# Encoder trunk with seven-product matmuls: a second buffer for a weight sum, three reordered steps, one low part moved from POOL to VectorE

## The reference

```python
h = _rmsnorm(x, g_ffn[l])
z = _dwconv_centred(h @ w_up[l], conv_w[l], conv_b[l])
z_gate, z_val = jnp.split(z, [D_FF], axis=-1)
x = x + (jax.nn.silu(z_gate) * z_val) @ w_down[l]
```

## Time and profile before

| what | before |
|---|---|
| median of 3 runs | 1118.75 us |
| the profiled execution's own time | 1118.39 us |
| its span | 1116.6 us |
| TensorE busy | 1081.9 us (97%) |
| VectorE busy | 640.1 us (57%) |
| ACT busy | 556.4 us (50%) |
| POOL busy | 623.5 us (56%) |
| DMA, mean over the span | 120 GB/s |

### The profile page before, as it was taken

One profiled execution on the slowest core, in us unless ns is written; L12 is line 12 of the kernel. 1 busy time (PEld: TensorE's weight loads), 2 busy tenths in 40 slices (PEclk: granted clock), 3 DMA queues, 4 the chain that ended last, 5 costly groups with the idle time before them and its releaser, 6 DMA issues.

```text
span 1116.6 us, 18354 instructions
## 1 busy us (share of the span) xinstructions
PE 1081.9 (97%) x6492; PEld 952.3 (85%) x6492; DVE 640.1 (57%) x938; ACT 556.4 (50%) x772; POOL 623.5 (56%) x298
## 2 busy tenths in 40 slices
PE   9999999999998999999999999999998989998997
PEld 7788888887988989998878888888888988898987
DVE  5726755675476723766636377467636665146564
ACT  7835444544465524665557344354434654255651
POOL 5343244355888668875524323344459775687840
PEclk9999999999999999999999999999999999999999
DMA  8222223233856356652623222223357642765312
GB/s 305 86 93 79 74 76 106 84 95 116 221 138 156 107 156 156 157 137 76 180 77 95 77 77 62 90 79 109 96 167 172 154 129 77 206 171 150 95 57 76
DMA packets 40549, 134.35 MB, mean 120 GB/s; under 512 B 4752, under 2 KB 7568, under 8 KB 40464
## 3 DMA queue, kind: packets, MB, share of 16 engines
q1 hardware_dynamic: 32848, 107.03, 29.6%
q0 software_dynamic: 6912, 25.17, 12.6%
q10 hardware_dynamic: 704, 1.07, 0.3%
HBM read 122.76 MB, written 2.10 MB: 112 GB/s over the span
## 4 chain that ended last, share of the span: by engine, by line
PE 60%; DVE 12%; DMA 8%; POOL 8%; issue 5%; ACT 4%; DVEq 1%; ACTq 0%; SPq 0%; POOLq 0%
PE acc L1479 12%; PE acc L1480 11%; PE acc L1481 11%; POOL w_lo L454 6%; PE acc L1793 4%; PE acc L1796 4%; PE acc L1795 4%; DMA w_raw<-mixer_sb 4%; DVE arena L1281 3%; PE acc L1605 3%; PE acc L1607 3%; PE acc L1606 3%; DMA mixer_sb<-mixer_sb 2%; DVE mixer_sb L1307 2%; DMA w_raw<-slabs 2%
## 5 line engine op out<-in xcount | busy, mean ns | idle before, releaser
L464 POOL TENSOR_TENSOR w_lo<-w_raw,w_hi 128x1024 fp32r<-128x1024 f32 x108 | 261.3, 2425 | 334.9 <-ACT w_hi L521 329.0
L454 POOL TENSOR_TENSOR w_lo<-w_raw,w_hi 128x1024 fp32r<-128x1024 f32 x72 | 182.3, 2572 | 73.2 <-ACT w_hi L804 60.7
L1479 PE MATMUL acc<-feat_hi,w_hi 128*128 128x512 f32 (+1 forms) x496 | 190.1, 383 | 1.5 <-DVE x L1223 1.5
L1480 PE MATMUL acc<-feat_lo,w_hi 128*128 128x512 f32 (+1 forms) x496 | 189.6, 382 | 0.0
L1481 PE MATMUL acc<-feat_hi,w_lo 128*128 128x512 f32 (+1 forms) x496 | 189.6, 382 | 0.0
L521 ACT ACTIVATE w_hi<-w_raw 128x1024 fp32r<-128x1024 f32 x102 | 107.8, 1063 | 139.8 <-PE acc L1481 103.4
L1793 PE MATMUL acc<-xg_hi,w_hi 128*128 128x256 f32 x512 | 145.9, 285 | 4.5 <-DVE sides L1329 4.5
L1795 PE MATMUL acc<-xg_lo,w_hi 128*128 128x256 f32 x512 | 145.7, 285 | 0.0
L1796 PE MATMUL acc<-xg_hi,w_lo 128*128 128x256 f32 x512 | 145.5, 284 | 0.0
L1479 PE MATMUL acc<-xg_hi,w_hi 128*128 128x512 f32 x352 | 139.6, 397 | 0.0
L1480 PE MATMUL acc<-xg_lo,w_hi 128*128 128x512 f32 x352 | 137.1, 389 | 0.0
(11 more groups left out here) (177 smaller groups left out, 2171.4 us busy)
## 6 DMA issues: line engine op xcount, KB each, us to landing
w_raw<-slabs SPq DMA_DIRECT2D x166, 512.0 KB, 3.5
w_raw<-slabs POOLq DMA_DIRECT2D x16, 512.0 KB, 5.8
arena<-slabs SPq DMA_DIRECT2D x16, 512.0 KB, 5.0
arena<-slabs POOLq DMA_DIRECT2D x16, 512.0 KB, 6.4
mixer_sb<-slabs SPq DMA_DIRECT2D x8, 512.0 KB, 5.5
w_raw<-mixer_sb POOLq DMA_DIRECT2D x8, 512.0 KB, 6.4
mixer_sb<-mixer_sb POOLq DMA_DIRECT2D x8, 512.0 KB, 5.6
outT<-arena SPq DMA_DIRECT2D x7, 256.0 KB, 2.2
```

The source lines that it names most:

```text
L454: pool.tensor_tensor(w_lo[:, w], source, w_hi[:, w].bitcast(F32), ALU.subtract).then_inc(lo_done, 1)
L464: pool.tensor_tensor(w_lo[:, w], w_raw[:, w], w_hi[:, w].bitcast(F32), ALU.subtract).then_inc(lo_done, 1)
L1479: pe.matmul(out, wh, ah, start=first, stop=False)
L1480: pe.matmul(out, wh, al, start=False, stop=False)
```

## The change

```diff
@@ sb
+        second_s2 = sb("second_s2", [P, SLAB])
-        s2_raw = mixer_sb[:, SLAB:2 * SLAB]
+        s2_raw = [mixer_sb[:, SLAB:2 * SLAB], second_s2[:, :]]
@@ POOL: add_s4, low_quad
-                pool.dma_start(raw2[s % 2], s2_raw, accum_op=ALU.add).then_inc(s4_added[s % 2], 16)
+                pool.dma_start(raw2[s % 2], s2_raw[s % 2], accum_op=ALU.add).then_inc(s4_added[s % 2], 16)
                 low(n + S1_, raw1[s % 2])
+                if s < KP - 1:
+                    add_s1(L, p, s + 1)
                 low(n + A11_, raw0[s % 2])
                 add_s3(L, p, s)
-                if s < KP - 1:
-                    add_s1(L, p, s + 1)
                 low(n + A12_, raw2[s % 2])
                 add_s4(L, p, s)
-                low(n + S2_, s2_raw)
-                low(n + A22_, raw(3))
+                low(n + S2_, s2_raw[s % 2])
+                low_done(n + A22_)
                 low(n + S3_, raw0[s % 2])
@@ ACT: quad_step
                     high_s3(p, s)
                     if s:
                         silu(p, s - 1, 1)
-                        feat_high(p, s - 1, 0)
                     high_s4(p, s)
                     if s:
-                        feat_high(p, s - 1, 1)
+                        feat_high(p, s - 1, 0)
                         act.wait_ge(c12_added, quad_at(p, s))
                     copy(p, s, S2_, 1, u2_copy)
                     if s < KP - 1:
                         high_s1(p, s + 1)
+                    else:
+                        high_down(p, 0)
+                    if s:
+                        feat_high(p, s - 1, 1)
+                    if s < KP - 1:
                         high_a11(p, s + 1)
                     else:
-                        high_down(p, 0)
                         high_down(p, 1)
                     copy(p, s, S3_, 1, u3_copy)
@@ VectorE: add_s2, low_a22, convolve, quad_step
-                    if p or s:
-                        before = p * KP + s - 1
+                    if p * KP + s > 1:
+                        before = p * KP + s - 2
                         dve.wait_ge(s4_added[before % 2], 16 * (L * (QUADS // 2)) + 16 * (before // 2 + 1))
-                    dve.tensor_tensor(s2_raw, raw1[s % 2], raw0[s % 2], ALU.add).then_inc(s2_done, 1)
+                    dve.tensor_tensor(s2_raw[s % 2], raw1[s % 2], raw0[s % 2], ALU.add).then_inc(s2_done, 1)
+
+                def low_a22(p, s):
+
+                    unit = first_unit(p, s) + A22_
+                    w = slice((unit % RING) * SLAB, (unit % RING + 1) * SLAB)
+                    dve.wait_ge(hi_done, L * NU + (unit + 1))
+                    dve.wait_ge(lo_done, L * NU + (unit + RING))
+                    dve.tensor_tensor(w_lo[:, w], raw(3), w_hi[:, w].bitcast(F32), ALU.subtract).then_inc(lo_done, 1)
@@ convolve
                     taps(p, s, 0)
+                    if s < KP - 1:
+                        low_a22(p, s + 1)
                     scale(p, s, 3)
@@ quad_step
                     else:
+                        low_a22(p, 0)
                         add_s2(p, 1)
```

More of the change, by code:

```diff
@@ L823, in high_s2 @@
                     act.wait_ge(s2_done, L * QUADS + (p * KP + s + 1))
-                    high(first_unit(p, s) + S2_, s2_raw)
+                    high(first_unit(p, s) + S2_, s2_raw[s % 2])
                 def high_a22(p, s):
```

## The result

| | before | changed |
|---|---|---|
| median | 1119.81 us (4 runs) | 1102.84 us (4 runs, 1101.76 to 1105.94) |
| the profiled execution, its span | 1118.39, 1116.6 us | 1102.49, 1100.7 us |
| TensorE, VectorE, ACT, POOL busy | 1081.9, 640.1, 556.4, 623.5 us | 1074.2, 634.0, 558.2, 586.5 us |
| the four parts together | 360.8 us | 344.5 us |

The ratio is 0.9846, 95% interval 0.9811 to 0.9881: **faster by 17 us**, 1.5%, where 3.8 us were forecast.

The account below looks back on a forecast made before the run. TensorE's waits in the four up-projection parts (360.77 us, 38.2 lost) bound it; a new 22.6 us circle would leave 356.95, so 1118.39 - 3.8 + 0.36 = 1115.0 us, range 1107 to 1128.

Parts of the forecast that it names:

- the waits at S3: TensorE's waits of 2.69 us at a quad's sixth product, behind u2_copy on ACT; claimed to go.
- a circle: Low S2 on POOL, low_a22, scaling, centring, p1_copy, S3, back to low S2: 22.6 us a quad against TensorE's 20.16.
- the walk: Times of each step counted from the end of POOL's low S2 to the next quad's low S2, 22.6 us.
- Then A11, A12 and S2, each behind one DMA issue: 3.61 each: Last steps of POOL's round, from 11.8 us after low S2 to 22.6, in every quad.
- Is the clock lowered after 2.45?: TensorE's clock after a 2.45 us wait at S2: a drop counted, costing 1.58 us, 0.45 coming back into the round.
- 0.6 late already: Third up-projection part: S2 of its first quad was claimed 0.6 us late, at 844.7.
- The round, 22.6: Time from one quad's S2 to the next's: at least 22.6 us, 23.05 after a clock drop.
- The handover: From POOL's end of low S2 to VectorE's low_a22: 0.15 us taken, between 0.08 and 0.32.
- The signs named in advance: S2 waits by L865, rounds of 22.6, VectorE idle before low_a22, add_s2 under 1.5, POOL some 38 less, last part 87 us.
- the waits simply go: First rival: with a round under 20.16 us TensorE would run through, 1080.5 us; chance 0.08.
- The second and third: Rivals: POOL's subtractions lock out add_s2, for the run (1147 us, chance 0.07) or one instruction (1128, chance 0.05).
- The rule weighed in the sum: POOL and VectorE share an SBUF read port, so moving A22's low part might not help; port use 18.0 to 16.8 us.

Follow-up runs that it names:

- old_s1_place: The changed kernel with the DMA add of S1 back at its old place, right behind add_s3: 1102.73 us, ratio 0.9866 to the kernel before.
- copy_before_centring: The changed kernel with p1_copy and S3's high part put ahead of the third centring on ACT: 1080.51 us, ratio 0.9665 to the kernel before.
- only_buffer: The kernel before with the second S2 buffer alone: 1108.88 us, ratio 0.9912.
- only_act_order: The kernel before with ACT's new order alone (u2_copy ahead of the second feature's high part): 1096.89 us, ratio 0.9824.
- a22_on_pool: The changed kernel with the low part of A22 back on POOL: 1095.75 us, ratio 0.9807 to the kernel before.
- best_a22_on_pool: The changed kernel with p1_copy and S3's high part ahead of the third centring, and A22's low part back on POOL: 1110.45 us.
- issue_in_last: The changed kernel with one more 64 KB DMA issued by POOL in each part's last quad: 1104.07 us, ratio 0.9875 to the kernel before.
- old_act_order: The changed kernel with ACT's old order, both high parts of the features ahead of u2_copy: 1109.85 us, ratio 0.9927 to the kernel before.

## Why the prediction was wrong

Its mechanism held: the waits at S3 went, a circle took their place at S2, every link in the order given, and cutting one link (two variants) made it vanish. So did the direction. The sum was 356.95 us for the parts and 344.5 was measured, 12.4 less, beyond the bounds given. So the steps that failed are terms of the walk and of the clock, not its path. Four were off, sized here by comparing the forecast starts of S2, from each part's start, with the measured ones:

1. **"Then A11, A12 and S2, each behind one DMA issue: 3.61 each", used for the last quad too: 4.5 us.** No S1 follows a part's last quad; the line `if s < KP - 1` stands in the diff. Nor does an `add_s2` meet S3 there. The last rounds took 21.3 to 21.6 us instead of 22.6: 1.3 in parts 2 and 4, 1.0 in parts 1 and 3. One walk was made for a quad "that has one before it" and used three times.
2. **"Is the clock lowered after 2.45? ... so I count 1.58": 3.9 us.** It fell after the waits of 2.45 and 2.43 us at S2 of the second quad in parts 1 and 3, which the walk had as 2.8 and, by its own starts (868.7 where TensorE would have been there at 864.98), as 3.7. It did not after those of 2.18 and 2.16 in parts 2 and 4, nor after the last ones of parts 1 and 3, 1.4 us, which the walk's long last round had made 2.45. That is two drops at a part's end (3.0) and twice 0.45 in a round. Interpolating between two rows was the error, more than its result (see the last section).
3. **Part 3 "0.6 late already": 1.9 us.** The part's first DMA for S1 landed 5.7 us after its issue, not 7.3 as before, and the part began like part 1. S1's new place isn't the reason, since old_s1_place shows the same. What sped the transfer up stays open.
4. **The round, 22.6 for 22.4, and the first S2 that waits in parts 1, 2 and 4, forecast 0.3 to 0.4 too late: 2.1 us together.** The handover took 0.03 us where 0.15 was taken, below the lower bound of 0.08: bounds from other pairs of engines weren't bounds for this one. S1's issue doesn't wait for POOL's own subtraction, so it adds 0.9 and not 1.2 (458.47 to 459.07 above has no 0.30 before it; the L478 has). Against these, `add_s2` put low S3 back by 0.24 and not 0.06.

The signs named in advance came out so: rounds of 22.4 and 21.3 us instead of 22.6; twelve waits at S2 released by L865; idle time before L1319 (1.82 us above; 26.4 behind POOL in 14 waits); no `add_s2` over 1.5 us; POOL less busy by 37.0 us, forecast 38. The last part took 85.07 us, not 87, which points at terms 1 and 2.

Of the rivals, the first ("the waits simply go") gave 1080.5 and needed a circle under 20.16 us. It has 1080.51 in copy_before_centring; the prediction saw the link that stood in the way but had no reason to weigh it as removable. The second and third, the lock-out of `add_s2`, did not happen in the changed kernel, because VectorE had only the taps in front, as argued. They happened in only_buffer, only_act_order, a22_on_pool and best_a22_on_pool, up to 12.7 us. On the third, the Trainium skill, SBUF — State Buffer, SBUF: two separate sides, has the one that started first hold the shared ports for one whole instruction: 3.35 us in only_act_order fit it, the 8.23 above do not.

The rule weighed in the sum, the Trainium skill's Perfetto Trace Analysis, Optimizing Scalar/DVE Operations (work moved between these two engines might bring nothing), doesn't settle it here: the same move costs 7 us in one order of ACT and brings 30 in the other. By these runs it depends on whether the piece falls into a pause of POOL and on what is queued behind it.

## What to carry to other kernels

When a piece of work moves to another engine behind a wait, follow what is queued behind it on that engine around until it comes back to whoever ends the wait; if the way round is longer than the period, cut it at the cheapest link, here by putting one copy and one high part ahead of a centring. Walk the first and the last turn of a loop by themselves, since guards such as `if s < KP - 1` take work out of them. And try each piece of a change alone and left out: here three pieces alone gave some 10, 6 and 20 us by their ratios, together 17, and with the circle cut 38.

## What the runs showed of the hardware

**VectorE can be kept out for a whole run of POOL's subtractions, and not only for one.** Over all fourteen traces 55 `add_s2` took more than 1.6 us. The 31 of up to 3.46 us met one subtraction. The 24 from 4.9 to 12.7 us met two to five, and every one of those began 0.2 to 0.37 us before the last had ended, as the rows at 317.40, 319.76 and 322.14 do. Two make 4.9 to 5.5 us, three 6.2 to 8.0, four 8.2 to 10.0, five 12.7. All 24 stood in a run without a pause behind a DMA issue of POOL. Most of the 31 were let in where POOL's next subtraction still had to wait, or where a DMA issue came next. But eight were not: there the next subtraction was free to go, and the sum got in ahead of it all the same. The rows of only_act_order above are one of them: ACT's high part, for which POOL's subtraction at 448.49 had to wait, was done at 447.52.

```profile
446.47 1.05 ACT L804 ACTIVATE w_hi<-mixer_sb 128x1024 fp32r<-128x1024 f32 x1
```

In those eight the run had begun, 0.04 to 1.1 us before the sum, with a subtraction that POOL itself had waited for. So a pause lets VectorE in, but a missing pause doesn't always keep it out; whether it is the DMA issue at the head of the run that does, no experiment here has tried.

**The length of a wait doesn't by itself decide whether TensorE's clock falls.** Two waits of issue_in_last, at S2 of the third quad in parts 2 and 4, and the 24 matmuls behind each; then two of old_act_order, in part 4 (columns of the stretches as above):

```profile
474.29 0.39 PE L1812 MATMUL acc<-t_hi,w_hi 128*128 128x256 f32 x1 [1.99 <-ACT arena L869]
1015.70 0.39 PE L1812 MATMUL acc<-t_hi,w_hi 128*128 128x256 f32 x1 [2.00 <-ACT arena L869]
...
474.29:478.75 4.46, 4.46 (x24) 4.46 (x25) 4.19 (x6) 2.84 (x4) 3.43 (x2) 0.62 0.30 111
1015.70:1018.67 2.97, 2.97 (x24) 2.97 (x25) 2.83 (x4) 2.85 (x4) 1.93 (x1) 1.00 0.44 163
```

```profile
1019.06 0.39 PE L1805 MATMUL acc<-t_hi,w_hi 128*128 128x256 f32 x1 [2.71 <-ACT arena L865]
1041.47 0.39 PE L1805 MATMUL acc<-t_hi,w_hi 128*128 128x256 f32 x1 [1.86 <-ACT arena L865]
...
1019.06:1022.03 2.97, 2.97 (x25) 2.97 (x26) 2.83 (x4) 2.55 (x4) 1.94 (x1) 1.00 0.34 134
1041.47:1045.93 4.46, 4.46 (x24) 4.46 (x25) 3.53 (x6) 3.44 (x5) 3.42 (x2) 0.62 0.14 53
```

Equal waits went both ways: a mean granted clock of 0.62 over the product after 1.99 us (between the 1.2 GHz level, 0.50, and the full one; 1.5 us lost), 1.00 after 2.00. The longer wait of 2.71 had no drop and the shorter of 1.86 had one. Over the fourteen traces, with the time from start to start counted as in the prediction, none of the 21 waits in the parts of 1.0 to 1.9 us had a drop; of the 46 from 1.94 to 3.6 us 29 had one and 17 had none; all six of 3.75 to 4.2 us had one. What else decides it, these runs don't show. A forecast should carry both outcomes for each wait of about 2 to 3.6 us, which lie 1.3 to 1.5 us apart in the product behind it (in four cases behind waits of 3.2 us and more, 2.1 to 2.3).
